# Recurrent stage: decay exponents as TensorE products with 0/1 matrices, 64x64 block products, and projections cut into half-projection slots

## What is computed

```python
f = lb + (1.0 - lb) * sigmoid(f_raw)          # lb is 0 here
log_f = log(maximum(f, TINY))                 # k = (1 - lb) * sigmoid(-f_raw), q = silu(q_raw) * 128 ** -0.5
def step(S, xs):
    qc, kc, gc, vc = xs
    G = cumsum(gc, axis=-2)
    o_inter = einsum('bhik,bhkv->bhiv', qc * exp(G), S)
    decay = exp(where(causal, G_i - G_j, NEG_BIG))
    A = einsum('bhik,bhijk,bhjk->bhij', qc, decay, kc)
    o_intra = einsum('bhij,bhjv->bhiv', A, vc)
    S_new = exp(G_last) * S + einsum('bhjk,bhjv->bhkv', kc * exp(G_last - G), vc)
    return S_new, o_inter + o_intra
# then rmsnorm over each head's 128 values, times onorm_w, times silu(g_raw)
```

## Time and profile before

| | |
|---|---|
| median of 3 runs | 1479.29 us (1478.36 to 1479.36) |
| profiled execution, its own time | 1479.96 us |
| its span, from the first to the last instruction | 1478.0 us |
| mean granted TensorE clock | 0.925 of full |
| TensorE busy | 1286.6 us (87%) |
| DVE, ScalarE, GpSimd busy | 754.0, 688.3, 426.4 us (51%, 47%, 29%) |
| half projections and other products of the recurrent stage | about 852 to 1040 us in the span |

### The profile page before, as it was taken

One profiled execution on the slowest core, in us unless ns is written; L12 is line 12 of the kernel. 1 busy time (PEld: TensorE's weight loads), 2 busy tenths in 40 slices (PEclk: granted clock), 3 DMA queues, 4 the chain that ended last, 5 costly groups with the idle time before them and its releaser, 6 DMA issues.

```text
span 1478.0 us, 17221 instructions
## 1 busy us (share of the span) xinstructions
PE 1286.6 (87%) x6104; PEld 981.2 (66%) x6104; DVE 754.0 (51%) x1466; ACT 688.3 (47%) x1262; POOL 426.4 (29%) x263
## 2 busy tenths in 40 slices
PE   5899999989799999879857777686879899999996
PEld 3577777767467776757535365665657788888884
DVE  4544454456746565745738665656675312121123
ACT  5566666652636776233455544454233223132231
POOL 2000000013200000422587651444323435344350
PEclk9999999999899999988868799688989999999998
DMA  4212222236132222522111000100433323323231
GB/s 154 97 58 86 72 72 73 85 116 211 51 93 80 78 72 72 185 72 79 43 43 57 1 29 29 57 29 29 173 140 143 128 86 100 100 85 114 84 102 57
DMA packets 36799, 126.93 MB, mean 86 GB/s; under 512 B 4448, under 2 KB 5216, under 8 KB 36720
## 3 DMA queue, kind: packets, MB, share of 16 engines
q1 hardware_dynamic: 33552, 119.81, 24.4%
q10 hardware_dynamic: 3168, 6.09, 1.4%
HBM read 122.44 MB, written 2.13 MB: 84 GB/s over the span
## 4 chain that ended last, share of the span: by engine, by line
PE 66%; issue 13%; DVE 11%; ACT 6%; POOL 3%; DMA 1%; DVEq 0%; ACTq 0%; POOLq 0%; SPq 0%
PE G L582 17%; PE G L584 17%; PE G L583 17%; DVE S L565 2%; POOL tmp L433 2%; PE S L761 1%; PE O L822 1%; PE T L801 1%; PE N L691 1%; PE S L1265 1%; PE S L882 1%; PE O L945 1%; PE T L929 1%; POOL wL L393 1%; ACT wH L1395 1%
## 5 line engine op out<-in xcount | busy, mean ns | idle before, releaser
L582 PE MATMUL G<-hi,wH 128*128 128x512 f32 x1360 | 570.1, 419 | 52.2 <-DVE lo L555 16.7
L393 POOL TENSOR_TENSOR wL<-w,wH 128x1024 fp32r<-128x1024 f32 x122 | 297.2, 2439 | 930.2 <-ACT wH L1395 930.1
L584 PE MATMUL G<-hi,wL 128*128 128x512 f32 x1360 | 542.2, 399 | 0.0
L583 PE MATMUL G<-lo,wH 128*128 128x512 f32 x1360 | 542.1, 399 | 0.0
L582 PEld LDWEIGHTS G<-hi,wH 128*128 128x128 f32 x1360 | 263.9, 194 | 133.6 <-issue 59.2
L583 PEld LDWEIGHTS G<-lo,wH 128*128 128x128 f32 x1360 | 264.7, 195 | 58.1 <-issue 7.8
L584 PEld LDWEIGHTS G<-hi,wL 128*128 128x128 f32 x1360 | 262.7, 193 | 58.1
L1395 ACT ACTIVATE wH<-w 128x1024 fp32r<-128x1024 f32 x170 | 179.1, 1054 | 167.9 <-PE G L584 134.8
L751 DVE CUSTOM_DVE_ANT_0 adaw<-adaw,scr 128x1024 f32<-128x1024 f32 x48 | 89.4, 1871 | 52.5 <-issue 52.5
L738 DVE SCALAR_TENSOR_TENSOR xT<-G,modT,xT 128x512 f32<-128x512 f32 x40 | 30.0, 749 | 134.8 <-PE G L584 134.8
L1751 DVE TENSOR_TENSOR wL<-w,wH 128x1024 fp32r<-128x1024 f32 x48 | 58.7, 1224 | 41.1 <-ACT wH L1395 40.4
(11 more groups left out here) (288 smaller groups left out, 1584.3 us busy)
## 6 DMA issues: line engine op xcount, KB each, us to landing
w<-weights_dram SPq DMA_DIRECT2D x170, 512.0 KB, 3.5
adaw<-ada_dram SPq DMA_DIRECT2D x48, 512.0 KB, 4.4
kd<-c_dram ACTq DMA_DIRECT2D x8, 512.0 KB, 3.5
xT<-x_dram SPq DMA_DIRECT2D x4, 512.0 KB, 5.9
out_dram<-xT SPq DMA_DIRECT2D x8, 256.0 KB, 2.2
scr<-ca_dram SPq DMA_DIRECT2D x2, 512.0 KB, 4.3
kd<-cbias ACTq DMA_DIRECT2D x8, 128.0 KB, 2.3
vb<-positions_dram SPq DMA_DIRECT2D x1, 256.0 KB, 8.3
```

What stands on the lines that cost most here:

```text
L393: g.tensor_tensor(wL[:, u.slot], w32[:, u.slot % 2], wH[:, u.slot].bitcast(f32), ALU.subtract).then_inc(w_lo, 1)
L582: mm(G[u.bank][:, :], whi, H[:, k, :], start=(k == first), stop=False)
L583: mm(G[u.bank][:, :], whi, L[:, k, :], start=False, stop=False)
L584: last = mm(G[u.bank][:, :], wlo, H[:, k, :], start=False, stop=(k == final))
```

## The change

- Steps: the scan and GpSimd's `differences` are gone. The gate's logarithm is transposed (`turn_g`) and clipped (`take_g`), and TensorE multiplies it, chunk by chunk, with eight 0/1 matrices (`diff`, `steps`), which gives the exponents in PSUM directly; ScalarE's exponential reads them there. The matrices are loaded by SP (three transfers, 0.5 MB) before unit UI+9.
- One operand a level: both halves of a level come from one DVE instruction (`operand`, with an access pattern over keys and queries), in four buffers.
- Products of 64x64: level m=64 is one 64x64 product for each chunk (`a0`, copied by ScalarE), the others two for each chunk, written to the two halves of the partitions. The predicated copies are 256 wide.
- Order: a **window** per head with 8 slots (`fill`), each of half a projection, between which the levels are spread; window 3's last slots hold parts of the first two output units. The four windows are written out, without a loop. The head's norm, the convolution's norm, the gates and the queries are put in pieces between the levels.
- Around it: the gate, value and query work of head 0 begins within the top-k search; copies of the transposed keys, the values and the matrix of level 64 go from DVE to ScalarE; the sum of the head's squares no longer shares its buffers.

```diff
+            def turn_g(t):
+                pe.wait_ge(sem("h_g"), t + 1 + since("h_g"))
+                if t:
+                    pe.wait_ge(sem("h_state"), 3 * t + since("h_state"))
+                for c in range(NQ):
+                    last = nc.tensor.transpose(T[0][:, c * P:(c + 1) * P], gl[:, c * P:(c + 1) * P], ident[:, :])
+                last.then_inc(sem("h_gturn"), 1)
+
+            def diff(t, j):
+
+                if j == KE:
+                    pe.wait_ge(sem("h_gT"), t + 1 + since("h_gT"))
+                if j in (2, 3):
+                    pe.wait_ge(sem("h_exp"), 9 * t + j + since("h_exp"))
+                elif j == 4:
+                    pe.wait_ge(sem("h_a0"), t + 1 + since("h_a0"))
+                elif j > 4 or t:
+                    pe.wait_ge(sem("h_aT"), (7 * t + j - 2 if j > 4 else 7 * t - 1 + j) + since("h_aT"))
+                for c in range(3 if j == KE else 4):
+                    last = mm(S[j % 2][:, c * P:(c + 1) * P], gT[:, c * P:(c + 1) * P], steps[j], start=True, stop=True)
+                last.then_inc(sem("h_diff"), 1)
...
+                    for b in range(2):
+                        at = slice(c * P + 64 * b, c * P + 64 * b + 64)
+                        last = mm(out_[64 * b:64 * b + 64, c, :], hk[:, at] if p < 2 else x[:, at],
+                                  hq[:, at] if p == 1 else x[:, at], start=True, stop=True)
...
+            def fill(t, k):
+
+                if t == 0:
+                    if k % 2:
+                        gemm_h(1, k // 4, [FIRST, SECOND][k // 2 % 2])
+                elif k < 4:
+                    gemm_h(t, 2 + k // 2, [FIRST, SECOND][k % 2])
+                elif t < 3:
+                    gemm_h(t + 1, k // 2 - 2, [FIRST, SECOND][k % 2])
+                else:
+                    if k % 2 == 0:
+                        output_m(k // 2 - 2, (4, 5))
+                        output_m(k // 2 - 2, (6, 7))
+                    else:
+                        output_m(k // 2 - 2, (0, 1))
+
+            def window(t):
+
+                diff(t, KE)
+                if t == 1:
+                    conv_sqsum()
+                fill(t, 0)
+                diff(t, QE)
+                diff(t, LV0)
+                if t:
+                    outputs(t - 1)
+                fill(t, 1)
+                diff(t, LV0 + 1)
+                turn_ke(t)
+                product(t, 0)
+                product(t, 1)
+                product(t, 2)
+                fill(t, 2)
+                diff(t, LV0 + 2)
+                turn_h(t)
+                if t:
+                    sum_h(t - 1)
+                product(t, 3)
+                fill(t, 3)
+                diff(t, LV0 + 3)
+                updates(t)
+                product(t, 4)
+                fill(t, 4)
+                diff(t, LV0 + 4)
+                product(t, 5)
+                fill(t, 5)
+                diff(t, LV0 + 5)
+                product(t, 6)
+                if t == 0:
+                    conv_sum()
+                fill(t, 6)
+                if t < 3:
+                    turn_g(t + 1)
+                product(t, 7)
+                fill(t, 7)
...
+            for t in range(4):
+                window(t)
+            output_m(0, (2,))
+            outputs(3)
+            output_m(1, (2,))
+            sum_h(3)
+            output_m(0, (3,))
+            output_m(1, (3,))
...
+            act.wait_ge(sem("i_acc"), 24)
+            forget(0)
+            split_h(0)
+            terms(CONV_CUTS[6], CONV_CUTS[7])
+            queries(0)
+            split_h(1)
+            terms(CONV_CUTS[7], CONV_CUTS[8])
...
+                    halves = here.rearrange("p (n a m) -> p n a m", a=2, m=m)
+                    v.tensor_tensor(halves, halves, kq_of(m), ALU.mult).then_inc(sem("h_x"), 1)
...
+            def window(t):
+                if t:
+                    queries_1(t)
+                operand(t, 0)
+                if t:
+                    joined(t - 1, 7)
```

More of the change, by code:

```diff
@@ L467, in head @@
-            def head(t, work=True):
-                for j in range(4):
-                    if work and j < 3:
-                        differences(t - 1, range(max(3 * j, 2), 3 * j + 3))
-                    split_lo(Unit(UH + AHEAD, j, t, 4))
-                    if not work:
-                        add_terms(CONV_CUTS[j + 6], CONV_CUTS[j + 7])
-                if not work:
-                    add_terms(CONV_CUTS[10], 60)
-                differences(t, (0, 1))
-            head(0, False)
@@ L479, in _ @@
-            repeated(pool, 4, head, first=1)
-            differences(3, range(2, 9))
+            for j in range(4):
+                split_lo(Unit(UH + AHEAD, j))
+                add_terms(CONV_CUTS[j + 6], CONV_CUTS[j + 7])
+            add_terms(CONV_CUTS[10], 60)
+            for j in range(4, 16):
+                split_lo(Unit(UH + AHEAD, j))
             for n in range(8):
@@ L1355, in _, with gemm_h @@
-            head(0, False)
-            attend_c()
-            turn_h(0)
-            head(1)
-            repeated(pe, 4, head, first=2)
-            states(3)
-            updates(3)
-            products(3, 0, 8)
+            def gemm_h(t, j, part=range(KT)):
+                free = [mark("h_raw2", t) if t else mark("i_raw", 12), mark("h_raw3", t) if t else mark("i_raw", 13),
+                        mark("h_klog", t + 1), mark("h_raw1", t + 1)][j]
+                gemm(pe, Unit(UH + 4 * t + j), hi2, lo2, free, part=part)
@@ new lines, in output_m @@
+            def output_m(n, part):
+                for name, count, tiles in (("c_gated_lo", 2, (4, 5)), ("cv_gated_lo", 2, (6, 7)), ("h_gated_lo", part[-1] + 1, (0, 1, 2, 3))):
+                    if part[-1] in tiles:
+                        pe.wait_ge(sem(name), count + since(name))
+                gemm(pe, Unit(UOM + n), hi1, lo1, mark(["h_raw2", "h_raw3"][n], 4), part=part, first=4, final=3)
+            def fill(t, k):
[12 more added lines that the diff above has]
+                        output_m(k // 2 - 2, (0, 1))
@@ L1373, in _ @@
+            output_m(1, (3,))
+            for n in range(2, 8):
+                gemm(pe, Unit(UOM, n), hi1, lo1, mark("x_m", n - 1))
             norm_tensor(pe, "mlp")
@@ L1715, in _ @@
+            split_h(3)
+            terms(CONV_CUTS[9], CONV_CUTS[10])
+            attend_c()
+            act.wait_ge(sem("conv_term"), 62)
+            keys(0)
+            act.wait_ge(sem("c_scores"), 16 + since("c_scores"))
+            decay(0, 0)
+            for t in range(4):
+                window(t)
+            square_h(3)
+            root_h(3)
             gated_h(3)
             for n in range(9):
-                if n < 8:
+                if 1 <= n < 8:
                     split_next(Unit(UOM, n))
@@ new lines, in states_of @@
+            def states_of(t):
+                dve.wait_ge(sem("h_update"), t + 1 + since("h_update"))
+                dve.wait_ge(sem("h_dec"), t + 1 + since("h_dec"))
+                wait(dve, sem("h_o"), t + since("h_o"))
+                v.tensor_copy(state[:, 0, :], T[0][:, 0:P]).then_inc(sem("h_state"), 1)
+                for c in range(1, 3):
+                    dve.wait_ge(sem("h_state"), t * 3 + c + since("h_state"))
+                    v.scalar_tensor_tensor(out=state[:, c, :], in0=state[:, c - 1, :], scalar=dec[:, c:c + 1],
+                                           in1=T[0][:, c * P:(c + 1) * P], op0=ALU.mult, op1=ALU.add).then_inc(sem("h_state"), 1)
@@ L2083, in _ @@
+            link(v.memset(scr[:, 512:768], 0.0))
+            dve.wait_ge(sem("conv_term"), 62)
+            take_g(0)
+            queries_2(0)
+            for t in range(4):
+                window(t)
+            joined(3, 7)
+            normed_h(3)
+            gated_h(3)
+            low_h(3)
             add_output(dve, "m", lambda n: Unit(UOM, n), 16, "mlp")
@@ L2188, in packed @@
     held["band"] = half(band)
+    at = np.arange(64)
     apart = np.where(at[None, :] > at[:, None], at[None, :] ^ at[:, None], 0)
-    held["level"] = np.stack([(apart >= 64 >> n) & (apart < 128 >> n) for n in range(7)], 1).astype(np.uint8)
+    levels = [(apart >= 32 >> n) & (apart < 64 >> n) for n in range(6)] + [at[None, :] == at[:, None]]
+    held["level"] = np.tile(np.stack(levels, 1), (2, 1, 1)).astype(np.uint8)
+    j, i = np.arange(P)[:, None], np.arange(P)[None, :]
+    parts = [j > i, j <= i]
+    for m in (64, 32, 16, 8, 4, 2):
+        mid = i // (2 * m) * (2 * m) + m
+        parts.append(np.where(i < mid, (j > i) & (j < mid), (j >= mid) & (j <= i)))
+    held["steps"] = np.concatenate(parts, 1).astype(np.float32)
     return held
```

623 lines of the change are left out of this document (336 added, 287 removed).

## The result

The changed kernel takes 1463.22 us (median of 4 runs, 1461.76 to 1465.23) against 1479.31 for the kernel before: ratio 0.989, 95% interval 0.988 to 0.991. It is faster by 16.1 us; 11.3 were forecast. The profiled execution took 1463.71 us, its span is 1461.9.

A forecast was written before the change was run, and what follows sets the result against it. A four-engine chain with idle time and half clock bounds the recurrent stage; afterwards TensorE's work nearly fills the windows. Stage -9.6 us (177.5 for 187.1, attention's loss included) and -1.7 behind give -11.3: 1468.0, forecast 1460 to 1475, range 1452 to 1485.

The forecast's parts named there:

- The bound: Recurrent stage: a chain of four engines, TensorE's own work under 34 us a round, the rest idle time and half clock.
- The block products: Windows: seven sets of eight 64x64 matmuls at 1.0 us and one of four at 0.5, 7.5 us a head.
- the row of 2 moving columns: Profile row, four matmuls with 128 stationary columns in 0.81 us: taken to show stationary loading as a set's floor.
- the row of 1.02 us: Profile row, 8 matmuls with 64 stationary and 128 moving columns: nearest row, upper end for a block-product set.
- Rival A: Windows: block products are cheap, 0.5 us a set, -23 us, 1456; chance 0.22, better still 0.05.
- The outputs: TensorE in a full window: 3 x 0.22 plus 12 with 64 moving columns at 0.20, 3.1 us (before 1.55).
- The transposes: TensorE in a full window: 11 transposed blocks at 0.09 us, 1.0 us.
- The half projections: TensorE in a full window: eight half projections of 12 matmuls at 2.85 us, 22.8 us.
- The idle time: Full window: 1.3 us idle before the second difference, 1.65 before the next gate's transposes; levels' round trips hidden.
- The attention: Before the windows: first exponentials 5.2 us later behind convolution terms, part regained, a 4.4 us loss; bounds 0 and 5.5.
- Behind the windows: After the last low half: adaLN blocks pace it; earlier transfer gains 2.4 us less 0.7, -1.7 in all.
- the unit ahead: Behind the windows: 0.7 us lost to the second unit's last matmuls; the 5.5 us computed ahead otherwise not seen.

The follow-up runs named there:

- doubled products: The changed kernel with each block product issued twice, 32 sets more: 1479.89 us, 1.0001 of the kernel before.
- gate first: The changed kernel with the next gate ahead of the convolution's gate arithmetic (window 1) and of a low half, on ScalarE and VectorE: 1460.59 us.
- split behind: The changed kernel with the weight split ahead of a window's last exponential moved behind the next window's first exponential: 1460.92 us.
- the experiment: The changed kernel with ScalarE's first weight split and four convolution terms ahead of the forget gate again, before the attention: 1463.96 us.
- products in turn: The changed kernel with all four 64x64 products of the first output half, then all four of the second, instead of alternating: 1468.64 us.

## Why the prediction was right, and where its terms were off

**The bound.** Right. The stage was a chain with half clock and is now TensorE's stream. The doubled products show it: some 15 us more work, 13.6 us more in the windows.

**The block products: the term that was most wrong.** I took 1.0 us a set between the ends 0.51 and 1.02, with the row of 2 moving columns as the floor: four matmuls with 128 stationary columns in 0.81. These products have 64 stationary columns, and then a matmul costs 0.11, half of it, and two in different halves overlap further to 0.058 to 0.076. The floor goes with the stationary columns, so the row with 128 of them wasn't the nearest one; the row of 1.02 us was, with its 64. A set is 0.61 between other work and 0.46 to 0.52 in the group of three: 4.6 us a window in place of 7.5. What the change of form costs shows in the neighbours: the differences ahead of such a set take 0.98 in place of 0.89. Rival A had this price nearly right. The Trainium skill, TensorEngine Tiling (Array Packing), Overview, gives up to 2x where the stationary side has 64 columns or fewer; the 0.90 against 0.61 us of the same eight matmuls shows that overlap, as 1.5x.

**And why the time wasn't rival A's.** Window 2 is the cleanest: 44.08 us with 2.1 idle, so 42.0 of work, where I had summed 42.9. The products bring 2.9 less, and other terms bring two thirds of it back. The outputs take 3.85 us (in window 3, 1025.46 to 1029.31) in place of 3.1: a matmul with 64 moving and 128 stationary columns lasts 0.224, as long as one with 128 moving, which is 0.3 of it; the rest are longer spacings where the pieces of this group meet. The transposes take 1.4 in place of 1.0 (four take 0.43 to 0.58, not 0.36), and the differences 7.1 in place of 6.9. In window 1 the long wait and the half clock behind it add some 4 us.

```profile
1005.77 0.69 PE L1279 MATMUL S<-kd 128*64 128x64 f32 x16
1006.38 0.50 PE L569 MATMUL G<-hi,wH 128*128 128x512 f32 x1
1006.72 0.40 PE L570 MATMUL G<-lo,wH 128*128 128x512 f32 x1
...
1026.49 0.38 PE L1312 MATMUL O<-scr,qkv 64*128 64x64 f32 x2
1026.72 0.38 PE L1311 MATMUL O<-scr,qkv 64*128 64x64 f32 x2
```

The half projections (2.85) were right, and this price already holds their slower first matmul (0.33 to 0.34 behind 64x64 products, 0.31 to 0.32 behind full f32 ones, in place of 0.23). So an error of 3 us a window and several of 2 us in sum nearly cancelled, which is luck.

**The idle time.** I said 1.3 us ahead of the second difference and 1.65 at the gate. The gate's wait was 1.3 in window 2 and 4.35 in window 1, where I had 3.0, and the start's wait was 0 to 0.8. The cause in window 1 was named in the prediction (the convolution's operations, GpSimd beside the last operand); two experiments took either away, and what is left of waits for a gate is at most 0.8 us (gate first) and 1.6 us (split behind). What I left out was the half clock, about 1.5 us a piece: behind the long wait in the changed kernel, and in other traces also where no long wait precedes it. By window: 29.5, 49.2, 44.1, 40.7 and 3.85 us, in sum 167.4, against 31.6, 47.6, 45.9, 41.1 and 3.8, in sum 170.0. All are within 2.1 us of the forecast, with both signs, and the sum is 2.6 low.

**The attention.** I forecast exponentials 5.2 us later; counted from the last relu they are 5.1 later (40.93 against 35.87). Then I gave back 0.8 to VectorE's normalising. Nothing came back: the four sets of exponentials are as far apart as before (36.03 and 36.04 from first to last), and behind the last another 0.8 is added. The shift is 5.9, not 4.4 and above my upper bound of 5.5. The cause that I named, the terms behind ScalarE's new order, holds the exponentials in the changed kernel. One half of it, the forget gate ahead of the split, is shown by the experiment (2.6 us). For the other half, the queries' operations, no run takes them away alone; and the copies in VectorE's search, which I had called free, would take their place at once.

**Behind the windows.** The third block's start, 5.7 us behind the low half by forecast, came 5.5 behind it (1042.95 against 1037.47). From there I took the pace of the old trace for granted, and counted the unit ahead as a loss of 0.7. It gave 2.5 us, and the earlier transfers 3.0. The step failed because I looked at one block only. Before, a pair of blocks took 3.3 and 1.2 us with 7.0 us from unit to unit; after, 1.2 and 2.1 to 2.4 with 5.84, as the block that waits for its transfer now begins over a us into GpSimd's split and no longer near its start (1056.22 against the split's 1056.03 before, 1051.69 against 1050.29 after).

```profile
1037.47 0.69 DVE L2191 TENSOR_TENSOR lo<-og,hi 128x512 fp32r<-128x512 f32 x1 [0.69 <-ACT hi L1750]
...
1042.95 1.63 DVE L738 CUSTOM_DVE_ANT_0 adaw<-adaw,scr 128x1024 f32<-128x1024 f32 x1 [1.81 <-issue]
...
1051.69 2.07 DVE L738 CUSTOM_DVE_ANT_0 adaw<-adaw,scr 128x1024 f32<-128x1024 f32 x1 [1.28 <-issue]
```

That this phase of splits and blocks is the reason is argued from the two traces; the experiments show only the sizes and that the DMA queue's order can move the stretch by 3.5 us.

**The sum.** +0.7 upstream, +5.9 in the attention, -16.5 from there to the last O, -5.6 behind the low half, -0.6 after the stage: -16.1. The forecast was 0, +4.4, -14.0, -1.7 and 0. The gain that was missed lies behind the windows (3.9) and in them (2.5), the loss that was missed in the attention (1.5). So the total is 4.8 us off, and it is that near in part because errors of both signs met.

## What to carry to other kernels

When a chain of engines is replaced by more work on the engine that is the bound elsewhere, sum that engine's work for one window first: if the sum nearly fills the window, it is the forecast, and a single badly priced term matters less than all small ones together. Price a matmul form by the row with the same number of stationary columns, and with what the change of form costs its neighbours: alone the 64x64 set was 0.2 us cheaper than the full one, in its place 0.07 to 0.09. Look for work that only happens to stand ahead of the next stage's first operation in an engine's queue (a low half, a split, another branch's arithmetic): moving four such pieces was worth 15 us here, nearly as much as the whole change.

## What the runs showed of the hardware

- f32 matmuls of 128 rows: 0.20 to 0.22 us with 128 stationary and 128 moving columns, 0.11 with 64 and 64 in one half of the output (0.14 in the short set of four), 0.058 to 0.076 where the halves alternate. A set of differences takes 0.89 us ahead of work with 128 stationary columns and 0.98 ahead of 64. With 64 rows, 128 stationary and 64 moving columns, 0.224, so fewer moving columns and rows gave nothing.
- The same window 0 took 32.79 us at a granted clock of 1.00 in three traces and 34.41 at 0.95 in two, window 1 49.24 at 0.97 and 50.8 at 0.93, with nothing changed in them. A wait of 4.35 us was followed by half clock; waits of 3.51 (products in turn) and 2.98 us (each product twice) were not, but a piece of half clock of some 4 us came in the next window. The stretch behind the stage, the same in all kernels, took 382.6 to 385.7 us. So one trace against another can't settle 3 us of this kernel; marks inside one trace can settle a few tenths.
- GpSimd and VectorE stretch each other: a 512-wide operand 2.49 us in place of 0.68 beside a split, and two splits 6.31 us in place of 4.8 beside the blocks.
